# Expert blocks of at most 64 rows in plain fp32 on column halves, paired with large blocks in an order worked out on the chip

## What is computed

```python
    def expert_block(args):
        xb, e = args
        hdn = jax.nn.silu(xb @ w_gate[e]) * (xb @ w_up[e])
        return hdn @ w_down[e]
```

## Time and profile before

| | us |
|---|---|
| median of three runs | 1358.87 (1358.85 to 1359.8) |
| the profiled execution | 1359.98 |
| its span | 1358.2 |
| PE busy | 1206.9 (89%) |
| VectorE busy | 844.2 (62%) |
| ScalarE busy | 701.9 (52%) |
| granted clock of PE, mean over the span | 0.935 |

### The profile page before, as it was taken

How to read it: one execution, slowest core, us unless ns; L and a number is a source line. 1 busy time by engine, 2 the same in 40 slices (tenths; PEclk the granted TensorE clock), 3 DMA queues, 4 the chain that set the end, 5 groups by cost and what they waited for, 6 DMA issues and landing times.

```text
span 1358.2 us, 18843 instructions
## 1 busy us (share of the span) xinstructions
PE 1206.9 (89%) x6923; PEld 1004.6 (74%) x6923; DVE 844.2 (62%) x1012; ACT 701.9 (52%) x889; POOL 240.5 (18%) x252
## 2 busy tenths in 40 slices
PE   4999999999889888899753999999999999999960
PEld 3899988999786566666543788888888888888850
DVE  5323233123435556675444789889888888988846
ACT  6212141134334444454331677777777787778730
POOL 4000002030200111000124122222222222222210
PEclk9999999999985889999865999999999999999985
DMA  8310015321121322221276799999999999999649
GB/s 245 94 63 1 1 57 183 134 96 32 64 85 41 91 70 76 76 79 62 77 319 238 281 384 374 382 387 386 385 378 383 375 374 381 378 385 387 262 152 367
DMA packets 66135, 291.44 MB, mean 215 GB/s; under 512 B 10600, under 2 KB 36232, under 8 KB 53536
## 3 DMA queue, kind: packets, MB, share of 16 engines
q1 hardware_dynamic: 48272, 243.91, 48.8%
q0 software_dynamic: 16656, 42.58, 8.4%
q10 hardware_dynamic: 1152, 4.19, 0.8%
HBM read 270.55 MB, written 37.92 MB: 227 GB/s over the span
## 4 chain that ended last, share of the span: by engine, by line
PE 81%; DVE 8%; DMA 4%; ACT 3%; issue 3%; SPq 1%; DVEq 0%; POOL 0%; POOLq 0%; ACTq 0%
PE ps L932 10%; PE ps L934 9%; PE ps L933 9%; PE ps L1201 9%; PE ps L1203 9%; PE ps L1202 9%; PE ps L1222 4%; PE ps L1224 4%; PE ps L1223 4%; PE ps L1013 3%; PE ps L1027 2%; PE ps L1190 2%; PE ps L1045 2%; DMA y<-expert_rows 2%; DVE probs L1800 2%
## 5 line engine op out<-in xcount | busy, mean ns | idle before, releaser
L1201 PE MATMUL ps<-wh,xh 128*128 128x512 f32 x512 | 205.1, 401 | 4.8 <-DVE xl L1866 4.8
L1203 PE MATMUL ps<-wh,xl 128*128 128x512 f32 x512 | 200.6, 392 | 0.0
L1202 PE MATMUL ps<-wl,xh 128*128 128x512 f32 x512 | 200.5, 392 | 0.0
L1866 DVE TENSOR_TENSOR wl<-wd,wh 128x2048 fp32r<-128x2048 f32 x64 | 143.8, 2288 | 31.1 <-ACT wh L1483 31.1
L1866 DVE TENSOR_TENSOR wl<-wu,wh 128x2048 fp32r<-128x2048 f32 x62 | 139.3, 2289 | 29.9 <-ACT wh L1483 28.0
L1866 DVE TENSOR_TENSOR wl<-wg,wh 128x2048 fp32r<-128x2048 f32 x64 | 143.9, 2289 | 10.0 <-ACT wh L1483 7.7
L1483 ACT ACTIVATE wh<-wg 128x2048 fp32r<-128x2048 f32 x64 | 118.9, 1909 | 7.4 <-PE ps L1203 7.4
L1483 ACT ACTIVATE wh<-wd 128x2048 fp32r<-128x2048 f32 x64 | 119.1, 1917 | 0.0
L1201 PEld LDWEIGHTS ps<-wh,xh 128*128 128x128 f32 x512 | 97.0, 190 | 29.6 <-DVE wl L1866 5.9
L1483 ACT ACTIVATE wh<-wu 128x2048 fp32r<-128x2048 f32 x64 | 118.7, 1906 | 0.0
L1203 PEld LDWEIGHTS ps<-wh,xl 128*128 128x128 f32 x512 | 96.7, 189 | 21.0
(11 more groups left out here) (300 smaller groups left out, 2635.8 us busy)
## 6 DMA issues: line engine op xcount, KB each, us to landing
wg<-in_w_gate SPq DMA_DIRECT2D x32, 2048.0 KB, 10.7
wu<-in_w_up SPq DMA_DIRECT2D x32, 2048.0 KB
wd<-in_w_down SPq DMA_DIRECT2D x32, 2048.0 KB
u_rows<-u POOLq DMA_DIRECT2D x16, 512.0 KB, 6.1
y<-expert_rows SPq DMA_DIRECT2D x16, 512.0 KB, 11.8
xin<-in_x SPq DMA_DIRECT2D x8, 512.0 KB, 8.2
zx<-in_x POOLq DMA_DIRECT2D x4, 1024.0 KB, 6.7
conv_part_rows<-zx POOLq DMA_DIRECT2D x16, 256.0 KB, 3.0
```

Source lines behind the costliest of these rows:

```text
L1201: mm(o, xh[:, k, :], wh[:, slot, k, :], start=(k == 0), stop=False)
L1202: mm(o, xh[:, k, :], wl[:, slot, k, :], start=False, stop=False)
L1203: last = mm(o, xl[:, k, :], wh[:, slot, k, :], start=False, stop=(k == KT - 1))
L1866: return V.tensor_tensor(dst, src, high_part.bitcast(F32), ALU.subtract)
```

## The change

**Small blocks.** A block of at most 64 rows is no longer split into high and low parts. PE multiplies in plain fp32, straight from the loaded matrices, with only 64 columns of the array in use: gate goes to the upper half of PSUM bank 7 and up to the lower half (`product_half`), and in `down_half` the two halves of the output go to the two halves of the array.

**Order.** The first two blocks are experts 0 and 1. The chip counts each free expert's rows, and works out on VectorE and PE (jobs `KIND` and `PLACE`) a place for each: first a loop of large blocks alone (0 up to `pairs_from`), then a loop of pairs, a large block at an even place with a small one at the odd place behind it. With these inputs `pairs_from` is 4 and the last pair is at 30: blocks 0 to 3 and the even ones from 4 to 30 are large form, the fourteen odd ones from 5 to 31 are small form.

**Buffers.** The low part of a matrix is now written over the matrix itself, in its slot, and the high part has one slot for each of gate, up and down. A slot is asked for again only when PE has used it (`done_with`). The first load behind experts 0 and 1, which was issued once the gate matrix of expert 0 was split, now waits for the gate product of block 0.

**Code order.** PE splits the gate product of the odd block around `turn_hidden`, and makes gate of block b + 2 before `down` of b + 1. VectorE and ScalarE follow.

```diff
@@ sync @@
-            def load_next(m, src, e, b, s):
-                sp.wait_ge(w_low[m], 2 * b - 2)
+            def load_matrix(m, e, b, s):
+                src = {"g": w_gate, "u": w_up, "d": w_down}[m]
+                sp.wait_ge(done_with[m][s], b // 2)
                 sp.dma_start(raw[m][:, s, :, :], src[e].rearrange("o (p k) f -> p (o k) f", p=P)
                              ).then_inc(w_in_sems[m][s], 16)
...
+            with sp.Fori(0, last - 2, 2) as i:
+                first, second = expert_of(i + 2), expert_of(i + 3)
+                load_matrix("u", first, i + 2, 0)
+                load_matrix("g", second, i + 2, 1)
+                load_matrix("u", second, i + 2, 1)
+                load_matrix("d", first, i + 2, 0)
+                load_matrix("g", expert_of(i + 4), i + 4, 0)
+                load_matrix("d", second, i + 2, 1)
@@ tensor @@
+            extra("KIND", 0)
+            extra("PLACE", 0)
...
+            def product_half(b, ks):
+                if ks[0] == 0:
+                    pe.wait_ge(x_taken, b + 2)
+                    for m in "gu":
+                        pe.wait_ge(w_in_sems[m][1], 8 * (b + 1))
+                for k in ks:
+                    for n, m in enumerate("gu"):
+                        last = mm(ps[HALF * n:HALF * (n + 1), 7, :], xa[:, k, :], raw[m][:, 1, k, :],
+                                  start=(k == 0), stop=(k == KT - 1))
+                        if k == KT - 1:
+                            last.then_inc(done_with[m][1], 1)
...
+            def down_half(b):
...
+                for k in range(FT):
+                    for j in range(2):
+                        last = mm(ps[HALF * j:HALF * (j + 1), 5 + j, :], ha[:, k, :], wd[:, 1, k, 512 * j:512 * (j + 1)],
+                                  start=(k == 0), stop=(k == FT - 1))
...
+            with pe.Fori(0, pairs_from, 2) as b:
+                product("g", b + 1, b + 1, 1, low_ks)
+                turn_hidden(b)
+                product("g", b + 1, b + 1, 1, high_ks)
+                product("u", b + 1, b + 1, 1)
+                turn_tokens(b + 2, 0)
+                down(b, b, 0)
+                turn_hidden(b + 1)
+                product("g", b + 2, b + 2, 0)
+                down(b + 1, b + 1, 1)
+                turn_tokens(b + 3, 1)
+                product("u", b + 2, b + 2, 0)
+            with pe.Fori(pairs_from, last, 2) as b:
+                nth = b // 2 + half_from
+                product_half(b + 1, low_ks)
+                turn_hidden(b)
+                product_half(b + 1, high_ks)
+                turn_tokens(b + 2, 0)
+                down(b, nth, 0)
+                turn_hidden(b + 1)
+                product("g", b + 2, nth + 1, 0)
+                down_half(b + 1)
+                turn_tokens(b + 3, 1)
+                product("u", b + 2, nth + 1, 0)
@@ scalar @@
+            with act.Fori(pairs_from, last, 2) as b:
+                take_x(b + 1)
+                high("g", b + 2, 0, (0, b // 2 + 1))
+                high_hidden(b)
+                silu_half(b + 1)
+                high_x(b + 2, 0)
+                high("u", b + 2, 0, (0, b // 2 + 1))
+                take_y(b, 0)
+                take_hidden(b + 1)
+                silu(b + 2, 0)
+                take_y_half(b + 1)
+                high("d", b + 2, 0, (0, b // 2 + 1))
@@ vector @@
+            with dve.Fori(0, pairs_from, 2) as b:
+                low_x(b + 1, b + 1, 1)
+                low("g", b + 1, 1)
+                low_hidden(b, b)
+                low("u", b + 1, 1)
+                hidden(b + 1, 1)
+                low_x(b + 2, b + 2, 0)
+                low("g", b + 2, 0)
+                low("d", b + 1, 1)
+                low_hidden(b + 1, b + 1)
+                low("u", b + 2, 0)
+                hidden(b + 2, 0)
+                low("d", b + 2, 0)
+            with dve.Fori(pairs_from, last, 2) as b:
+                nth = b // 2 + half_from
+                low("g", nth + 1, 0)
+                low_hidden(b, nth)
+                hidden_half(b + 1)
+                low_x(b + 2, nth + 1, 0)
+                low("u", nth + 1, 0)
+                hidden(b + 2, 0)
+                low("d", nth + 1, 0)
```

More of the change, by code:

```diff
@@ L63 @@
 TABC = STEPS * NE
+TABW = TABC + 8
 VC = (AW + H) // 2
@@ L695, in _ @@
+            first, second = expert_of(last), expert_of(last + 1)
+            load_matrix("u", first, last, 0)
+            load_matrix("g", second, last, 1)
+            load_matrix("u", second, last, 1)
+            load_matrix("d", first, last, 0)
+            load_matrix("d", second, last, 1)
+            for s in range(2):
+                sp.wait_ge(done_with["g"][s], last // 2 + 1)
             sp.wait_ge(h1_out, 16 * NT)
@@ L1237, in _ @@
-            turn_tokens(0, 0)
-            product("g", 0, 0, True)
-            product("u", 0, 1, False)
-            turn_tokens(1, 1)
-            with pe.Fori(0, final, 2) as i:
-                for s in range(2):
-                    blocks(i + s, s, True)
-            blocks(final, 0, False)
-            turn_hidden(final + 1)
-            down(final + 1, 1)
+                            mm(o, hh[:, k, :], wh["d"][:, r, :], start=(k == 0), stop=False)
+                            mm(o, hh[:, k, :], wl["d"][:, s, r, :], start=False, stop=False)
@@ new lines, in _ @@
+            low_ks, high_ks = range(KT // 2), range(KT // 2, KT)
+            turn_tokens(0, 0)
+            product("g", 0, 0, 0)
+            turn_tokens(1, 1)
+            product("u", 0, 0, 0)
+            wait_x_used(pe, ("PLACE", 0))
+            pe.wait_ge(route_ready, 1)
+            pairs_from = pe.value_load(plan[0:1, 0:1], min_val=2, max_val=LAST)
+            half_from = pe.value_load(plan[0:1, 1:2], min_val=1, max_val=LAST // 2)
+            last = pe.value_load(plan[0:1, 2:3], min_val=4, max_val=LAST)
@@ L1249, in _ @@
+            turn_hidden(last)
+            product_half(last + 1, high_ks)
+            down(last, last // 2 + half_from, 0)
+            turn_hidden(last + 1)
+            down_half(last + 1)
         @block.scalar
@@ L1521, in _, with take_y_half @@
[L1521 to L1531 removed]
+            def take_y_half(b):
+                act.wait_ge(done_with["d"][1], b // 2 + 1)
+                act.wait_ge(yb_free, b + 1)
+                then(A(yb[0:HALF, 1, 0:512], ps[0:HALF, 5, :], ACT.Copy))
+                A(yb[0:HALF, 1, 512:], ps[HALF:, 6, :], ACT.Copy).then_inc(y_taken, 1)
@@ L1922, in _ @@
-            low_x(0)
-            low("g", 1, 1, 0)
-            hidden(0)
-            low_x(1)
-            with dve.Fori(0, last, 2) as i:
-                for s in range(2):
-                    blocks(i + s, s, True)
-            blocks(last, 0, False)
-            low_hidden(last + 1)
-            low("d", last + 1, 1, 1)
+                rest("g", 0, n)
+            job = ("PLACE", 0)
+            wait_x_made(dve, job)
+            V.tensor_scalar(rowf[:, :], ps[0:1, x_bank(job), 0:COLS], float(TABC), None, ALU.add).then_inc(x_used, 1)
```

404 lines of the change are left out of this document (241 added, 163 removed).

## The result

The changed kernel takes 1366.02 us (median of 20 runs, 1354.81 to 1374.73) beside 1358.6 for the kernel before (20 runs, 1354.35 to 1360.23). The ratio is 1.005, 95% interval 1.0031 to 1.0068: slower by half a per cent, and more scattered from run to run. The profiled execution has a span of 1364.2 us against 1358.2.

A forecast was written before the change was run, and what follows sets the result against it. PE and the DMA engines (98% busy) were both nearly full, and DMA was taken to bound the changed pairs. First blocks +28, pairs -14.5, end -9.4, POOL's fill +0.4 sum to +4.5: 1363 us, range 1356 to 1371.

The forecast's parts named there:

- A small block is 24 plain fp32 matmuls at 0.43, 10.3 us: Small blocks on PE: column halves run at once, so gate, up and down take 10.3 us in place of 16.3.
- Rival 3: Small blocks: halves do not overlap at 512 columns, a pair takes 40 us on PE, total 1443; chance 0.05.
- PE's path of a pair is 32.0, with a wait of 2.4: Pair loop: 29.6 us of PE work plus 2.4 waiting at `down` for VectorE, where loads keep up.
- First four blocks +28: All-large blocks 0 to 3: PE waits for VectorE and ScalarE, plus lower clock and register reads, 96.4 us against 68.3.
- Rival 2: First blocks: half of the 28 us of early stalls does not come, total 1349; chance 0.15.
- Thirteen pairs -14.5: Block 4 to 30: 13 pairs of 34.9 us less 5 for slots loaded early, 448.7 against 463.2.
- 98% busy in 35.63 us leaves a pair at 34.9: Pair loop: the old DMA busy share sets a pair at 34.9 us, 2.9 above PE's path.
- rival 4: Pair loop: clock falls in every pair, hidden under 34.9 unless loads then start late; 13 x 2.3 more, 1393; chance 0.08.
- End -9.4: Block 30 to the last matmul: 38.0 us of work and some 7 of waits, 45 against 54.4.
- POOL's fill +0.4: Before the first gather: POOL's extra fill of eight table columns adds 0.4 us.
- Rival 1: Pair loop: DMA follows PE, moving faster than 420 GB/s; pairs of 32.0 us, total 1331; chance 0.12.
- The sentence on the swizzle: Pair loop: rows on partitions 0 to 63 load only half of the sixteen DMA engines, giving 34.4 us a pair.

The follow-up runs named there:

- x6: Changed kernel with small-block matmuls no longer alternating between column halves; a small block takes 15.5 us for 10.3, the stretch from block 4 to 30 13.4 us longer.
- x11: Changed kernel loading only half of each of the three weight matrices of blocks 7, 9, ... 29; after the first pair, twelve pairs of 32.2 us.
- x1: Changed kernel with VectorE's split of the even block's down matrix moved behind the next up split in the all-large loop; ratio 0.998 to the kernel before.
- x10: Changed kernel with VectorE's down split later, ScalarE's token copy and VectorE's register reads earlier, odd blocks' rows on partitions 64 to 127; 1331.9 us.
- x5: Changed kernel with 16 useless identity transposes on PE ahead of each small block's product, filling its wait for tokens; ratio 1.0035 to the kernel before.
- x7: Kernel before, with block 2's gate load and the loads behind it held back until block 1's token rows are gathered; 1355.3 us.
- x12: Kernel before, with those loads held back behind the tables and the rows of all blocks from block 2 on spread over 128 partitions; 1354.7 us.
- x9: Changed kernel with the rows of odd blocks from block 3 on moved to partitions 64 to 127; stretch from block 4 to 30 fell 23.8 us to 432.5.

## Why the prediction was right, and where its terms were off

The forecast of 1363 (own range 1356 to 1371) and its sign held; the sum of +4.5 was measured as +6.0 in the profile and +7.4 in the medians. That the sum came so close is in part luck: +3.0 in the first four blocks, +7.7 in the pairs and +1.7 behind the last matmul stand against -4.0 at the end and -7.0 ahead of block 0. Of the signs named for a right forecast, 389 GB/s, the idle time at the first plain fp32 matmul (33.6 us in 11) and the wait for VectorE at L1241 (8.5) were there. The DMA share was 0.94, not 0.98 or more; even blocks lay 32.2 to 37.5 us apart, not 34 to 35; and blocks 2 and 4 lay 54.7 apart, not 49. The terms:

- *A small block is 24 plain fp32 matmuls at 0.43, 10.3 us.* Right (the rows at 1100 us). Rival 3 is out, and x6 shows that the overlap is robust: it costs 5 us a block, not 10, had the turns been given up.
- *PE's path of a pair is 32.0, with a wait of 2.4.* Measured 32.2 with a wait of 1.5 (x11): two misses of about 1 us that cancel. Of the 1.1 us more of work, 0.5 are the changes between halves and whole array that the sum had left out. (By the forecast's own figures, 10.4 and 0.3 against 8.0, the wait would have been 2.7.)
- *First four blocks +28.* Measured +31.0. The two stalls for the gate split are 8.6 and 8.5 (8.9 forecast). The 2 us more for register reads did not come: they passed behind the down split, and appear only where that split is gone (x1, 2.06). Up's two are 2.2 each (2.3), `hl` 2.1 (2.4). Together these are 23.5 us. PE is busy 73.4 us for the same matmuls that took 63.4 before, at a clock of 0.81 for 0.93: the clock cost 10 us, not 4.6, since it fell at the waits of 2 us too. The waits for `xl` are 2.3 shorter. x1 takes 8.6 of the 31 away and x10 12.3; the rest is waits of the same kind and their clock, and no run removed it. Rival 2 is out.
- *Thirteen pairs -14.5.* Measured -6.8, the term that failed, by 7.7 us. Two steps of it: "98% busy in 35.63 us leaves a pair at 34.9", and rival 4's "still hidden under 34.9". The eleven pairs from block 8 on last 35.3 on average, 4.2 us more in all. The first two take 68.2, where 64.8 were forecast: the reserve of 5 us was counted, but not that the first pair holds block 3's large `down` (1.7) and loses 1.5 to the clock. In the others a wait for the loads does not simply stand in the place of idle DMA time. The lower clock comes behind it; the slots, freed by PE's products, come free later, and the DMA engines are idle more (share 0.94, not 0.98). The clock's some 15 us are measured; that late slots pass them on to the loads is argued. With the wait filled (x5) the stretch is 448.7; that this is the forecast's own number is chance. So rival 4 was part of the truth: the miss is half of the forecast gain, and a quarter of the 30 us that this rival had.
- *End -9.4.* Measured -13.4: in the last blocks PE waits 1.2 us (39.81 busy of 41.00), not 7.
- *POOL's fill +0.4.* The fill takes 0.1 us and the step behind it 0.3, as forecast. Missed was that block 0 starts 6.6 us earlier, 5.7 of them before the slot table's load is issued, a good part of it scatter from one execution to the next. The load of block 2's gate matrix is now issued behind the slot table and the gathers; x7 prices that at 2.7 in the old kernel.
- *Behind the last matmul* 1.7 more; not studied.

Rival 1 (loads at over 420 GB/s, pairs of 32.0, 1331) did not happen in the change as made. But the reading of the earlier trace rows as a limit of the DMA engines, "98% busy in 35.63 us leaves a pair at 34.9", was wrong in kind, and that the mean pair came out at 35.1 doesn't confirm it. The changed kernel moves 389 GB/s at a share of 0.94, and x10 moves 414 at 1.00: the same 414 for a full share, where the old kernel's rows give 389 (381 at 0.98). The place of the rows is not what made that old rate, for x12 spreads them and stays at 382 at 0.98. What the place changes, by the shares, is how much of the time engines stand idle: 0.94 became 0.98 in x9. The sentence on the swizzle, which the prediction gave as an estimate beside its sum, pointed to the fix, though its 34.4 a pair did not come (35.1): x9 is worth 1.7% of the changed kernel's time (ratio 1.005 to 0.9883).

The change is thus worth having with its surroundings mended: x10 against x12, both with tables first and rows in better places, is 1331.9 to 1354.7.

## What to carry to other kernels

When PE time is taken out of a kernel whose DMA engines are 98% busy, don't take the share for the bound, and ask whether all sixteen are loaded alike: moving one stream of rows from partitions 0 to 63 to the other 64 was worth 23 us, more than the 20 that the small blocks had gained in the pairs and at the end. Between an engine's waits in program order, put first what is ready (the tokens), and behind it what waits for a load; and put no split ahead of the operand for which PE stands still. A wait on PE can cost more than its length: after 2 to 4.5 us of waiting, 1.5 to 2.7 more mostly went to the lower clock, so a forecast "hidden under the loads" has to include how late the slots then come free.

## What the runs showed of the hardware

- Matmuls on two column halves overlap beyond neighbours: with eight records on one half and then eight on the other, the second half's first starts as the first's fifth does, and twelve steps of 0.43 us do for sixteen records (x6).
- The weight loads' packets themselves took 7% less time per byte in the changed kernel. In the DMA part from 860 to 1260 us, first of the kernel before and then of the changed one:

```profile
q1 hardware_dynamic: 9673, 140.92, 90.4%
```

```profile
q1 hardware_dynamic: 9901, 144.27, 86.3%
```

140.92 MB in 90.4% of 400 us are 390 GB/s, 144.27 in 86.3% are 418; x12, the old kernel with spread rows, stays at 393. What differs is VectorE's and ScalarE's work (411 and 363 us busy of 463, and 225 and 226 of 456); whether their reads slow the packets was not tried. So a busy share near 1 was no measure of what the engines could carry.
- The changed kernel's runs scatter by 20 us, the old one's by 6. Its pairs fall into those of 32.2 and those of 34 to 37.5, and x1, whose pair loop is the same, has them in other places; that small shifts of a load decide which is a guess.
